# Squares of the latents moved from GpSimd to ScalarE and VectorE, and a new order of work between head pairs

## The reference, cut to what matters

```
h = rms_norm(x) * (1 + scale) + shift
xr, gr, qc, kvc, kr, ga = split(h @ w_in)     # 1024, 1024, 512, 512, 64, 1024 columns
y_rnn = rg_lru(conv4(xr)) * silu(gr)          # gates: block-diagonal 64x64 products
q  = rms_norm(qc) @ w_uq;   kv = rms_norm(kvc) @ w_ukv     # 8 heads
q_nope, k_nope: rms_norm per head;  q_pe, k_pe: rms_norm, then rotary turn; k_pe shared
s  = (q_nope k_nope^T + q_pe k_pe^T) / sqrt(192), causal;  o = softmax(s) v
x + gate * (concat(y_rnn, o * silu(ga)) @ w_out)
```

## Time and profile before

| | |
|---|---|
| median of 3 runs | 2243.2 us (2243.05 to 2244.1) |
| the profiled execution's own time | 2244.95 us |
| its span | 2243.4 us |
| PE busy | 2181.7 us, 97% of the span |
| DVE, ACT, POOL busy | 1298.9, 756.0 and 109.1 us |
| granted clock of PE, mean | 0.99 |
| DMA | 294.44 MB, mean 131 GB/s |

### The profile page before, as it was taken

How to read it: one execution, slowest core, us unless ns; L and a number is a source line. 1 busy time by engine, 2 the same in 40 slices (tenths; PEclk the granted TensorE clock), 3 DMA queues, 4 the chain that set the end, 5 groups by cost and what they waited for, 6 DMA issues and landing times.

```text
span 2243.4 us, 27236 instructions
## 1 busy us (share of the span) xinstructions
PE 2181.7 (97%) x9790; PEld 1734.3 (77%) x9790; DVE 1298.9 (58%) x2140; ACT 756.0 (34%) x997; POOL 109.1 (5%) x144
## 2 busy tenths in 40 slices
PE   7999999999999999999989999989999998999999
PEld 5888888878788888887778888868877777666787
DVE  5566867667676767777752323252237886556333
ACT  5232423223242322324242212252234445554111
POOL 0000000000000000000000000000000401100000
PEclk9999999999999999999999999989999999999999
DMA  6555555545555454655363423333332322112332
GB/s 209 176 155 158 155 153 169 156 135 180 148 159 162 148 168 124 195 148 174 129 211 118 149 96 132 124 130 97 94 92 66 98 82 77 33 48 69 121 120 93
DMA packets 213856, 294.44 MB, mean 131 GB/s; under 512 B 16074, under 2 KB 150114, under 8 KB 212642
## 3 DMA queue, kind: packets, MB, share of 16 engines
q1 hardware_dynamic: 200722, 256.12, 36.8%
q0 software_dynamic: 8624, 29.04, 4.7%
q10 hardware_dynamic: 4448, 8.45, 1.0%
HBM read 273.51 MB, written 20.05 MB: 131 GB/s over the span
## 4 chain that ended last, share of the span: by engine, by line
PE 93%; DVE 4%; ACT 1%; issue 1%; DMA 1%; SPq 0%; DVEq 0%; ACTq 0%
PE ps L2225 27%; PE ps L2227 27%; PE ps L2226 27%; PE ps L2308 2%; PE ps L2560 1%; PE ps L2312 1%; PE ps L2315 1%; PE ps L2580 1%; PE ps L2558 1%; DVE w_lo L1672 1%; PE ps L2471 1%; PE ps L2322 1%; PE ps L2297 1%; PE ps L2561 1%; DMA xt<-in_x_dram 1%
## 5 line engine op out<-in xcount | busy, mean ns | idle before, releaser
L2225 PE MATMUL ps<-hn_hi,w_hi 128*128 128x512 f32 x1280 | 522.2, 408 | 0.8 <-DVE hn_lo L1424 0.8
L2227 PE MATMUL ps<-hn_hi,w_lo 128*128 128x512 f32 x1280 | 505.6, 395 | 0.0
L2226 PE MATMUL ps<-hn_lo,w_hi 128*128 128x512 f32 x1280 | 505.3, 395 | 0.0
L1672 DVE TENSOR_TENSOR w_lo<-w_raw,w_hi 128x1024 fp32r<-128x1024 f32 x174 | 215.6, 1243 | 422.6 <-ACT w_hi L1062 421.0
L1062 ACT ACTIVATE w_hi<-w_raw 128x1024 fp32r<-128x1024 f32 x174 | 183.6, 1058 | 491.3 <-PE ps L2227 449.2
L1414 DVE TENSOR_TENSOR w_lo<-w_raw,w_hi 128x1024 fp32r<-128x1024 f32 x162 | 198.0, 1222 | 247.5 <-ACT w_hi L937 246.7
L937 ACT ACTIVATE w_hi<-w_raw 128x1024 fp32r<-128x1024 f32 x162 | 171.3, 1058 | 427.4 <-PE ps L2227 417.2
L2225 PEld LDWEIGHTS ps<-hn_hi,w_hi 128*128 128x128 f32 x1280 | 240.2, 188 | 61.9 <-issue 7.7
L2226 PEld LDWEIGHTS ps<-hn_lo,w_hi 128*128 128x128 f32 x1280 | 240.2, 188 | 61.2 <-issue 6.7
L2227 PEld LDWEIGHTS ps<-hn_hi,w_lo 128*128 128x128 f32 x1280 | 239.9, 187 | 58.9
L2225 PE MATMUL ps<-w_hi,y_hi 128*128 128x512 f32 x512 | 206.2, 403 | 7.5 <-DVE y_lo L1681 7.5
(11 more groups left out here) (366 smaller groups left out, 2749.6 us busy)
## 6 DMA issues: line engine op xcount, KB each, us to landing
ada_raw<-in_w_ada_dram SPq DMA_DIRECT2D x128, 384.0 KB, 3.4
w_raw<-in_ssm_w_in_dram SPq DMA_DIRECT2D x96, 512.0 KB, 4.6
w_raw<-in_ssm_w_in_dram SPq DMA_DIRECT2D x128, 256.0 KB, 3.8
w_raw<-in_w_in_dram SPq DMA_DIRECT2D x64, 512.0 KB, 3.8
w_raw<-in_ssm_w_out_dram SPq DMA_DIRECT2D x60, 512.0 KB, 3.9
csb<-cs_rows POOLq DMA_DIRECT2D x32, 512.0 KB, 5.9
w_raw<-in_w_out_dram SPq DMA_DIRECT2D x32, 512.0 KB, 3.7
y_rows<-yt POOLq DMA_DIRECT2D x8, 1024.0 KB, 8.3
```

The source lines that it names most:

```text
L1672: nc.vector.tensor_tensor(w_lo[:, slot, :], w_raw[:, slot, :], w_hi[:, slot, :].bitcast(F32), ALU.subtract).then_inc(lo_ready, 1)
L2225: nc.tensor.matmul(out_, a_hi, b_hi, start=start, stop=False)
L2226: nc.tensor.matmul(out_, a_hi, b_lo, start=False, stop=False)
L2227: return nc.tensor.matmul(out_, a_lo, b_hi, start=False, stop=stop)
```

## The change

- POOL no longer squares. ACT squares four pieces at once (128x2048) into `gr[:, 0:4]`, after its splits of slots 0 and 2 of the first `ga` units; DVE adds the four pieces in two steps after its splits of slots 1 and 3. The second square waits for the first sums, since both use the same memory. `c_hi(0)` waits for both sums. POOL's loads of gate weights become one loop with the same wait.
- PE turns the rotary keys and sums the squares after one `ga` panel, not two. DVE's work on the rotary keys and the mean comes after two panels, not three; the root is asked for there and taken back after three.
- `make_c_lo` moves from behind the split of unit 2 to in front of `lru_logs` in unit 1.
- In front of the first pair's scores DVE takes its sums of q's squares and two splits before the copy of the turned keys; PE does `tile(1, 1)` before it turns k.
- Between pairs PE does `tile(g+1, 1)` before the last `head_sum`, and turns q's rotary part before `tile(g+1, 2)`, not after it; ACT copies it before it reads that tile. In the last such place two output tiles stand in for the missing tiles, and their left sides are made earlier; two tiles fewer follow later.

```diff
@@ POOL
-            with pool.Fori(0, NT + 1) as j:
+            with pool.Fori(0, RNN_BLOCKS) as j:
                 load_gates(j)
-            pool.wait_ge(f_bank_freed, 2 * (RNN_PANELS + QKV_PANELS + 1))
-            pool.wait_ge(rnn_done, NT)
-            for part in range(2):
...
@@ ACT
-                            act.wait_ge(latent_added, 1)
+                            act.wait_ge(latent_added, 2)
                             make_c_hi(i)
...
                 split_hi(U_GA + u, u, landed_before(U_GA) + 1)
+                if u in (0, 2):
+                    part = u // 2
+                    if part:
+                        act.wait_ge(latent_added, part)
+                    else:
+                        act.wait_ge(rnn_done, NT)
+                        act.wait_ge(f_bank_freed, 2 * (RNN_PANELS + QKV_PANELS + 1))
+                    nc.scalar.activation(gr[:, 0:LORA_KB, :], qkvc[:, part * LORA_KB:(part + 1) * LORA_KB, :], ACT.Square
+                                         ).then_inc(latent_squared, 1)
...
+                act.wait_ge(pe_turned, g + 2)
+                nc.scalar.activation(qpt[:], ps[:, QPE_BANK, :], ACT.Copy).then_inc(qk_ready, 1)
                 if g + 1 < PAIRS:
                     read_tile(g + 1, 2)
-                act.wait_ge(pe_turned, g + 2)
-                nc.scalar.activation(qpt[:], ps[:, QPE_BANK, :], ACT.Copy).then_inc(qk_ready, 1)
...
                     if cur and k in (6, 7):
                         pair_hi(g * 4 + k)
+                        if g + 1 == PAIRS:
+                            make_y2_hi(k - 6)
@@ DVE
+                        if unit == U_GA and u == 1:
+                            make_c_lo(i)
                         if lru is not None and u == 1:
                             lru_logs(gb, n)
-                        if unit == U_GA and u == 2:
-                            make_c_lo(i)
...
                 split_lo(U_GA + u, u)
+                if u in (1, 3):
+                    part = u // 2
+                    dve.wait_ge(latent_squared, part + 1)
+                    st.done(nc.vector.tensor_tensor(gr[:, 0:2, :], gr[:, 0:2, :], gr[:, 2:4, :], ALU.add))
+                    st.wait()
+                    nc.vector.tensor_tensor(latent_sq[part], gr[:, 0, :], gr[:, 1, :], ALU.add
+                                            ).then_inc(latent_added, 1)
...
-            panels(U_GA, 3, 4)
+            panels(U_GA, 2, 4)
             dve.wait_ge(kr_turned, 1)
...
             dve.sem_inc(root_asked, 1)
+            panels(U_GA, 3, 4, first=2)
             dve.wait_ge(root_done, NT + 4)
...
                     if cur and k == 7:
                         pair_lo(g * 4 + 6)
+                        if g + 1 == PAIRS:
+                            make_y2_lo(0)
...
                 head_out(p, 0)
+                if g + 1 == PAIRS:
+                    make_y2_lo(1)
                 keep_prob(p, 6)
...
-            dve.wait_ge(kpe_turned, 1)
-            nc.vector.tensor_copy(kpt[:], ps[:, 5, :]).then_inc(kpt_ready, 1)
             q_sums(0)
             for n in range(4, 6):
                 pair_lo(n)
+            dve.wait_ge(kpe_turned, 1)
+            nc.vector.tensor_copy(kpt[:], ps[:, 5, :]).then_inc(kpt_ready, 1)
             k_sums(0)
@@ PE
-            panels(3, U_GA, 2, 4)
+            panels(3, U_GA, 1, 4)
             turn_kr()
             sum_latents()
-            panels(3, U_GA, 4, 4, first=2)
+            panels(3, U_GA, 4, 4, first=1)
...
-                        out2_tiles((1, 2, 2, 2, 2, 2, 1, 1)[k])
+                        out2_tiles((1, 2, 2, 2, 1, 1, 1, 1)[k])
...
                 elif not cur:
                     out2_tiles(2)
+                elif cur:
+                    out2_tiles(1)
                 turn_prob(p, 7)
+                if g + 1 < PAIRS:
+                    tile(g + 1, 1)
+                elif cur:
+                    out2_tiles(1)
                 head_sum(p, 1)
...
             def turn_rest(g):
-                if g + 1 < PAIRS:
-                    tile(g + 1, 1)
                 turn_k_tok(g)
+                turn_qpe(g)
                 if g + 1 < PAIRS:
                     tile(g + 1, 2)
-                turn_qpe(g)
...
             tile(1, 0)
+            tile(1, 1)
             pe.wait_ge(kpt_ready, 1)
```

More of the change, by code:

```diff
@@ L308, in build_program @@
         lc = sb("lc", [P, 8], F32, scope_f)
-        latent_sq = sb("latent_sq", [P, SEQ], F32, scope_f)
+        gd_sq = sb("gd_sq", [P, SEQ], F32, scope_f)
         scope_f.close()
@@ L351, in build_program @@
         scope2.close()
+        latent_sq = (gd_sq[:], gr[:, 3, :])
         def y2_block(b, low):
@@ L487, in build_program @@
         kr_ready = sem("kr_ready")
+        latent_squared = sem("latent_squared")
         latent_added = sem("latent_added")
@@ L1290, in turned @@
                     read_tile(g + 1, 1)
-                else:
-                    for b in range(2):
-                        make_y2_hi(b)
                 act.wait_ge(k_turned, g + 1)
@@ L2132, in scores @@
                     pair_lo(g * 4 + 7)
-                    if g + 1 == PAIRS:
-                        for b in range(2):
-                            make_y2_lo(b)
                 else:
@@ L2501, in sum_latents @@
                         mm = nc.tensor.matmul(ps[:, 6, part * NT + t:part * NT + t + 1],
-                                              gr[:, 2 + part, t * P:(t + 1) * P], ones[:, 0:1], start=True, stop=True)
+                                              latent_sq[part][:, t * P:(t + 1) * P], ones[:, 0:1], start=True, stop=True)
                     mm.then_inc(latent_summed, 1)
-            panels(3, U_GA, 2, 4)
+            panels(3, U_GA, 1, 4)
             turn_kr()
             sum_latents()
-            panels(3, U_GA, 4, 4, first=2)
+            panels(3, U_GA, 4, 4, first=1)
             def turn_kpe():
```

## The result

The changed kernel took 2232.43 us (median of 5 runs, 2228.44 to 2233.74), the kernel before 2243.47 beside it (5 runs, 2243.05 to 2244.78). The ratio is 0.9946 with a 95% interval of 0.9932 to 0.9961, so 0.5% faster; the forecast of 2230 lies inside the spread of the runs and 2.4 us from their median. The profiled execution took 2233.74 us, with a span of 2232.2.

What follows compares the result with a forecast made beforehand. PE, busy 97% of the span, bounds the kernel; only its 20.3 us of waits and slow clock can be won. 3.6 - 2.0 + 1.0 - 0.4 + 0.6 + 6.1 + 4.4 + 0 = 13.3 us gives 2230 us, range 2226 to 2236.5.

Steps and rivals of the forecast that it cites:

- Part 1: First two gates: without POOL's squares the second gates' 3.57 us wait goes, +3.6; the first gates' wait becomes 2.6, -2.0.
- Part 2: Last two latent gates: moving the keys' work and root ends the fourth gates' wait, +1.0; new third-gates wait, -0.4.
- Part 3: First q tile's wait for `c_lo(3)` goes, +1.4; tile 4 then waits for the last `c_lo`, -0.8.
- Part 4: Before the first scores: 3.9 us wait, 2.6 slow clock and 1.2 `qpt` wait go, 1.9 wait comes; +6.1 with edges.
- rival B: Clock falls after the new 1.9 us wait before `turn_k_tok`, 2.6 us lost, 2232.6 us; chance 0.15.
- Part 5: Between pairs: after pairs 0 and 1 tiles fill waits of 0.86 and 1.2 us, +2.2 each; after pair 2, net 0.
- What would make it wrong: First gates waiting over 5 us, or the clock's low level showing in more than one place.
- rival D: Clock falls at all four places where transposes stand together and stays down; 2257 us with 54 us low; chance 0.04.
- Rival A: Turns of ACT and DVE cost more: 2.6 us more lost at the first gates, 2232.6 us; chance 0.13.
- C: Order after pair 2 better than forecast, clock holds, first gates lose only 1.0 us: 2227 us; chance 0.10.
- E: Before the scores the new order saves nothing because weights hold the splits: 2236 us; chance 0.10.

## Why the prediction was right, point by point

- **Part 1, +3.6 - 2.0.** That POOL's squares caused the 3.57 us wait is shown by taking three quarters of them away. The wait at the first gates was 2.15, 0.45 less than worked out; it cost 1.35 more than before. The step that failed is that nothing but the wait was priced there: the clock fell behind it and cost 1.6 to 1.7 more, shown by freeing the squares. So Part 1 brought 0.8 and not 1.6: with the squares alone moved, gates 3 come at 86.43 and not 87.21. With the 3.0 lost at the first gates, the gain at the second is 3.8 by difference, near the 3.6. In the kernel after, where the keys' work has also come in, they stand at 87.28.
- **Part 2, +1.0 - 0.4.** The fourth gates lost their wait (+1.0). The new wait at the third was 0.77, and 0.9 with its edges: moving the keys' work behind the convolution took it away (gates 2 to 3 in 24.1, not 25.0). The slack was as forecast. The work was put too low, at 2.0: between DVE's split and the convolution it held DVE for 2.3 (1826.91 to 1830.33, against 1800.59 to 1801.72 in the panel without it).
- **Part 3, +1.4 - 0.8.** Panel 4 to the first q tile gained 1.6, tile 4 gave back 0.9, or 1.0 with its edges: right. No run undid this part alone.
- **Part 4, +6.1.** 6.3 measured between the turned keys and pair 0's first score. The wait of 1.80 and the full clock came as forecast, and rival B did not happen. It was near: with a wait of 2.11 there, in the run with the longer third wait, the clock did fall, for 1.6 of the 1.9 us lost, the other 0.3 being the wait itself. The 2.6 for the slow clock came from one execution: the 18 slow matmuls of the kernel before were ten in the three other traces with the same 3.9 us wait, and by those the part would have brought 1.2 less.
- **Part 5, twice +2.2 and 0.** 2.57 a pair, 0.4 more than the 2.2 forecast; undoing it returns 2.5 and 2.6. Behind pair 2, the next score came 2.57 later and 2.78 less followed, so net +0.2, and the kernel with the fill undone has it at -0.1: 0 was right, and so was its reason, since with the 2.70 us wait gone 4.2 us came free, 2.7 of wait and 1.5 of clock and edges.
- **The sum** of 13.3 met 13.2, in part by luck: by gates 3, 1.3 was lost that was not foreseen (0.8 in Part 1, for the clock, and 0.5 at the third gates), and 0.7 between pairs 0 to 2 and 0.2 each in Part 4 and behind pair 2 came back.
- **What would make it wrong** was put too sharply, and it happened: the clock was low at more than one place (the first gates, which was not foreseen, and behind pair 2, which was). The forecast held all the same, since such a spell costs 1.6 us, not the tens that rival D needed, and other parts made it up. Rival A's price (2.6 more lost at the first gates, from dearer turns) came to 1.0 by another way (1.7 of clock, and the wait 1.35 dearer where 2.0 was forecast). Rivals C, D and E did not occur.

## What to carry to other kernels

An engine that shares nothing in the program with a busy one can still slow it: look at the same instruction in two stretches before counting work. Where an edit makes a wait on TensorE, price the low clock behind it as well as the wait: the 2.15 and 2.70 us waits here were worth 4.0 and 4.2 us when they were taken away whole. When engines take turns over one buffer, try a second one, with the work that hangs on it moved off the path: the two together were worth 4.0 here, the moved squares 0.8.

## What the runs showed of the hardware

- The clock fell behind gate waits of 2.06 to 2.25, 2.14, 3.52 and 3.70 us, in three different panels, and stayed full behind 0.77, 0.97 and 1.15, but also behind the 3.57 us of the kernel before, the one exception. A rough difference is that the window of its wait shows DMA traffic during the wait and the others' hardly any (share 0.51 here, 0.05 in the kernel after at 1778.30 to 1780.40); that this is the cause was not tried, and it stays open. At the same panel the 3.70 us wait, behind which it fell, has a share of 0.00, which fits. But traffic alone does not hold the clock: during the wait of 2.11 before `turn_k_tok` the share was 0.79, and the clock fell behind it. The last of these lines is that wait.

```profile
1801.40:1805.00 3.60, 0.08 (x1) 0.00 (x0) 3.34 (x7) 2.34 (x2) 0.00 (x0) 1.00 0.51 131
```

```profile
1778.30:1780.40 2.10, 0.02 (x1) 0.00 (x0) 2.03 (x4) 2.02 (x2) 0.00 (x0) 1.00 0.05 17
```

```profile
1901.60:1903.60 2.00, 0.00 (x0) 0.00 (x0) 1.93 (x6) 1.05 (x3) 0.00 (x0) 1.00 0.79 265
```

- Behind the same wait the low spell can be long, short or missing: six slow matmuls or ten behind 4.14 us in two executions of one kernel, and between kernels that do not differ at the place 18 or ten behind 3.9 us, and 4.12 or 2.42 us for eight matmuls behind 1.55. Whether edits 100 us ahead had a part in the last two is not shown. So an experiment on one wait must be read in the stretches between anchors; in the total, 1 to 3 us of clock hide what the edit did.
- POOL's arithmetic on 128x512 squares made DVE's splits of 128x1024 take 2.07 and not 1.18 us, and its rotation made two of them take 3.29 and not 2.35.
